# Row length of two normalised operand tiles in a float32r transformer step, 386 or 392 floats

## The reference

```python
def trunk(x, c, p):
    for li in range(DEPTH):                       # DEPTH = 2
        sh1, sc1, g1, sh2, sc2, g2 = ada_mods(c, p['w_ada'][li], p['b_ada'][li])
        h = rms_norm(x, p['norm_w'][li, 0]) * (1 + sc1) + sh1
        y = even_layer(h, ...) if li % 2 == 0 else odd_layer(h, ...)
        x = x + g1 * y
        h = rms_norm(x, p['norm_w'][li, 1]) * (1 + sc2) + sh2
        x = x + g2 * (jnp.square(jax.nn.relu(h @ p['w_mlp1'][li])) @ p['w_mlp2'][li])
```

## Time and profile before

| | |
|---|---|
| Median of 3 runs | 1049.16 us |
| Runs | 1047.77 to 1050.31 us |
| Span of the profiled execution | 1047.8 us |
| Its time outside the span | not shown by the page |
| PE busy in the span | 1020.6 us, 97% |
| DVE, ACT, POOL busy | 568.5, 486.1, 140.8 us |
| DMA | 160.44 MB, mean 153 GB/s |
| TensorE clock granted, mean | 0.994 |

### The profile page before, as it was taken

How to read it: one execution, slowest core, us unless ns; L and a number is a source line. 1 busy time by engine, 2 the same in 40 slices (tenths; PEclk the granted TensorE clock), 3 DMA queues, 4 the chain that set the end, 5 groups by cost and what they waited for, 6 DMA issues and landing times.

```text
span 1047.8 us, 17863 instructions
## 1 busy us (share of the span) xinstructions
PE 1020.6 (97%) x7330; PEld 941.7 (90%) x7330; DVE 568.5 (54%) x914; ACT 486.1 (46%) x858; POOL 140.8 (13%) x173
## 2 busy tenths in 40 slices
PE   6999999999999999999999999999999999999997
PEld 3888885778999999999997989886999999999997
DVE  5556676564744345354457576576465445345452
ACT  5544665664553342342344556667464234252342
POOL 0162200011010010110110342350001011010110
PEclk9999999999999999999999999998999999999999
DMA  9987719645435445445445532223223524333311
GB/s 330 343 283 244 237 48 322 202 162 195 152 121 167 155 161 161 161 159 162 153 129 186 176 104 68 86 87 101 80 81 121 162 92 149 120 120 120 121 41 61
DMA packets 156974, 160.44 MB, mean 153 GB/s; under 512 B 3146, under 2 KB 155108, under 8 KB 156900
## 3 DMA queue, kind: packets, MB, share of 16 engines
q1 hardware_dynamic: 154512, 156.15, 45.0%
q0 software_dynamic: 704, 1.97, 0.6%
q10 hardware_dynamic: 1684, 1.26, 0.4%
HBM read 156.09 MB, written 3.28 MB: 152 GB/s over the span
## 4 chain that ended last, share of the span: by engine, by line
PE 92%; DVE 3%; ACT 2%; issue 1%; DMA 1%; SPq 0%; DVEq 0%; ACTq 0%
PE G L585 63%; PE G L590 13%; PE OB L607 4%; PE TB L554 4%; PE SC L918 2%; PE OB L932 1%; PE SC L694 1%; DMA raw<-in_w_ada 1%; PE OB L715 1%; PE OB L785 1%; PE TB L900 1%; ACT wH L1024 1%; PE SC L670 1%; PE SC L664 1%; PE SC L626 1%
## 5 line engine op out<-in xcount | busy, mean ns | idle before, releaser
L585 PE MATMUL G<-opH,wH 128*128 128x386 f32 (+1 forms) x768 | 267.7, 349 | 1.1 <-DVE wL L1505 0.8
L1024 ACT ACTIVATE wH<-raw 128x2048 fp32r<-128x2048 f32 x94 | 179.6, 1911 | 180.9 <-PE G L585 178.1
L585 PE MATMUL G<-opH,wL 128*128 128x386 f32 (+1 forms) x768 | 260.4, 339 | 0.0
L585 PE MATMUL G<-opL,wH 128*128 128x386 f32 (+1 forms) x768 | 260.2, 339 | 0.0
L1505 DVE TENSOR_TENSOR wL<-raw,wH 128x2048 fp32r<-128x2048 f32 x94 | 215.8, 2296 | 42.9 <-ACT wH L1024 42.9
L585 PE MATMUL G<-hidH,wH 128*128 128x384 f32 x512 | 173.3, 338 | 0.0
L585 PE MATMUL G<-hidH,wL 128*128 128x384 f32 x512 | 172.1, 336 | 0.0
L585 PE MATMUL G<-hidL,wH 128*128 128x384 f32 x512 | 172.1, 336 | 0.0
L585 PEld LDWEIGHTS G<-opH,wH 128*128 128x128 f32 x768 | 144.9, 189 | 9.8 <-issue 5.4
L585 PEld LDWEIGHTS G<-opL,wH 128*128 128x128 f32 x768 | 144.8, 189 | 1.6
L585 PEld LDWEIGHTS G<-opH,wL 128*128 128x128 f32 x768 | 144.9, 189 | 0.0
(11 more groups left out here) (246 smaller groups left out, 1192.6 us busy)
## 6 DMA issues: line engine op xcount, KB each, us to landing
raw<-in_w_mlp SPq DMA_DIRECT2D x64, 1024.0 KB, 5.2
raw<-in_w_ada SPq DMA_DIRECT2D x48, 1024.0 KB, 7.0
raw<-in_w_in_even SPq DMA_DIRECT2D x13, 1024.0 KB, 7.2
raw<-in_w_in_odd SPq DMA_DIRECT2D x12, 1024.0 KB, 5.1
raw<-in_w_out_even SPq DMA_DIRECT2D x4, 1024.0 KB, 6.6
raw<-in_w_out_odd SPq DMA_DIRECT2D x4, 1024.0 KB, 5.0
xin<-in_x_sample SPq DMA_DIRECT2D x2, 512.0 KB, 5.7
out_y_sample<-yout SPq DMA_DIRECT2D x1, 768.0 KB, 4.1
```

Source lines behind the costliest of these rows:

```text
L585: mm = pe.matmul(G[:, s, 512 * m:512 * m + cols], w[:, s, k, P * m:P * m + P], a[:, k, 0:cols], start=first and q == 0, stop=last and q == 2)
L1024: act.activation(wH[:, u % 2, :, :], raw[:, pos % RAW, :, :], ACT.Copy).then_inc(w_high, 1)
```

## The change

The two tiles get rows of 392 floats, 1568 bytes, which is 49 times 32. Every row of `opH` and `opL` then begins at a multiple of 32 bytes. The last six floats of a row are never written or read. `opL` begins 192 bytes later than before, all that is declared behind it 384 bytes later. No instruction is added or removed, and no shape changes.

```diff
 NX = NTOK + 2
+ROW = 392
...
-        opH = sb("opH", [P, KT, NX], F32R)
-        opL = sb("opL", [P, KT, NX], F32R)
+        opH = sb("opH", [P, KT, ROW], F32R)
+        opL = sb("opL", [P, KT, ROW], F32R)
```

## The result

The changed kernel takes 1052.2 us, the median of 20 runs (1050.26 to 1055.1), against 1049.39 us for 20 runs of the kernel before beside it (1045.38 to 1053.25): a ratio of 1.0028, 95% interval 1.0019 to 1.0038. It is slower by 2.9 us, where 1045.0 was forecast. Its profiled execution has a span of 1048.1 us.

The account below looks back on a forecast made before the run. TensorE, busy 97% of the span, was taken as the bound through the pace between matmul starts. Gains of 1.8 + 0.8 + 1.6 = 4.2 us took 1049.2 to 1045.0 us, range 1042.7 to 1047.4.

Parts of the forecast that it names:

- pieces of 32 bytes: Matmul pace on TensorE: a streamed row costs 3.61 ns for each 32-byte piece it touches, taken from `hid` rows.
- Three paces that agree within 0.7 ns: Measured `op` paces the assumption fitted: 175.7 ns at 384 columns, 177.2 and 177.6 at 386 in layers 1 and 0.
- the sentence that was called its refutation: Irregular steps in the 384-column output projection units of the changed trace would make the prediction wrong at its root.
- Item 1: 768 matmuls of 384 columns out of `op`: from 175.7 to 173.3 ns each, a gain of 1.8 us.
- Item 3: 1224 tok matmuls, stationary tile coming into phase: half of the possible gain taken, 1.6 us.
- Item 2: 1536 matmuls of 386 columns: from 177.4 to 176.9 ns each, a gain of 0.8 us.
- Item 5: Later tiles move by 384 bytes, a multiple of 32, 64 and 128, so their phases stay: no effect.
- locked at the bad end: Rival, 386-column units: steps repeat at 180 ns instead of 177.4, costing 4.0 us less 1.8, giving 1051.4; chance 0.12.

Follow-up runs that it names:

- e3_pads: Kernel before, rows of 386 floats kept, with 192 unused bytes behind each of `opH` and `opL`; ratio 1.0001 to the kernel before.
- e12: Changed kernel with `opH`/`opL` rows 28 bytes past a multiple of 32 and `raw` 192 past a multiple of 256; ratio 0.9952 to the kernel before.
- e1: Model left out: blocks of 96 or 144 matmuls alone at various row places, a `hid` block returning between; ran once, `hid` at 173.3 or 176.7 ns.
- e2: Changed kernel with layer 1's MLP rows taken in layer 0's order, nothing else; ratio 1.0001 to the kernel before.
- e8: Model left out: matmul blocks alone, 392-float rows at eight phases, also rows of 386, 388, 390; 386 columns took 173.9 to 177.9 ns.

## Why the prediction was wrong

The bound was read rightly: TensorE's pace sets the time, and neither the other engines nor the two tiles' writers gave or took anything (`opL` 554 ns and `opH` 528 as before). The forecast failed at three steps.

**Its root: pieces of 32 bytes.** Three paces that agree within 0.7 ns were taken for a law, from one assumption and four measured numbers. The blocks alone contradict it, and the sentence that was called its refutation came true: the 384-column output units, in phase at every row, stand at 175.3 ns with uneven steps (172 to 185), not at `hid`'s 173.3. Item 1 gave 0.4 ns x 768 = 0.3 us instead of 1.8. Item 3 gave nothing: tok went from 118.2 to 118.4, a loss of 0.2 us where 1.6 were forecast. Item 2 came out as forecast by luck: from the first matmul of each group of 386-column units to the next group's, layer 0 gained 144.54 - 143.88 = 0.66 us and layer 1 138.73 - 138.64 = 0.09, 0.75 against 0.8, but for another reason, since e3_pads gains 1.6 with the old rows. The upper end of the range was off as well: its gain of 6.5 us is no sum of the items, which give 1.8 + 0.8 + 3.2 = 5.8 with all of tok's.

**Item 5, "Nothing".** The later tiles keep their phases of 32, 64 and 128, and that was where the reasoning stopped; `raw` stood on a multiple of 256 and left it. The trace of before shows `raw` filled at 386 GB/s with the DMA engines full in the prologue, the one place where TensorE's waits are put down to it, so it was a term to be bounded and not one to be struck out. It costs some 1.5 to 2 us. The Trainium skill, page "DMA: Bandwidth & Descriptors", section "How a descriptor splits into AXI transactions", says that a descriptor which does not start on a multiple of 256 bytes is split at those multiples, and that the bytes between the multiple below and its start cost as well. It speaks of what is read; here it is the place written to that moved. By its figures a 1 KB packet that starts 128 bytes past takes 36 beats instead of 32, an estimate of 343 GB/s from 386; 348 was measured, close to it. 192 bytes past it would be 38 beats and 325 GB/s, and e12 shows 348, so the trace does not agree with the figures there. By the same account both places cut a packet into one more piece than before; whether that sets the rate is not shown.

**Item 5 again: `hid` left out.** The prediction took `hid`'s 173.3 ns as what rows in phase cost, a constant. It is one of two patterns of the same instructions at the same addresses, and what runs ahead can choose between them (e1, e2). The change turned layer 1 into the other: 2.1 us, the largest term of the result beside the prologue, and no part of the sum. The rival "locked at the bad end" had the mechanism, steps that repeat at a slow value, and the right side, but put it into the 386-column units, at 180 ns; those went to 176.7. That its time, 1051.4, lies near the 1052.2 measured is luck: the loss came from other terms. The 180 ns exist (388 columns, rows of 512 floats) where no kernel here uses them.

**The sum as it came out:** a gain of 0.75 + 0.3 - 0.2 = 0.85 us in the changed units, a loss of 2.1 in `hid` and about 2 in the prologue: some 3.2 us slower, where the runs show 2.9, between 2.0 and 4.0.

**Still open.** Why a place and an entry give one pattern and not another was not found: distances between tiles, the weights' place and the rows' order all enter, and the opening blocks of e1 and e8 differ with all of these equal. Why the clock falls in some executions is open too. Of the runs with `raw` off its multiple 69 of 72 have a mean granted clock of 0.995 or less, of those with `raw` on it, the kernel before among them, 68 of 115; 0.993 or less have 51 of the 72 and 10 of the 115. So the fall comes oftener with the late transfers, but it comes without them too, and how the price of some 2 us divides between the wait and the clock was not measured.

## What to carry to other kernels

Where TensorE streams without a gap, a tile's place in SBUF is a parameter to be measured and not one to be reasoned out: run the matmuls alone at the eight phases of a row, take the fastest, and look in the model whether the streams behind it keep their pattern. Whoever changes one tile's size should list every tile declared behind it with its old and new place, up to multiples of 512 bytes, and ask of those that DMAs fill whether they left a multiple of 256. A constant read from the profile is only one where something shows that it cannot be otherwise; `hid`'s pace was the same in every undisturbed unit before, and was still one of two.

## What the runs showed of the hardware

- One stream of matmuls at the same addresses runs at 173.33 or 176.67 ns a step, depending on the block ahead of it, and once settled stays so to the end of the block, of 96 matmuls (e1: L29, L35, L37). With no block ahead it settled at either pace as well (e1 L27, e8 L34).
- Neither alignment nor fewer columns is a guide to the pace: 388 columns at 180.0 ns against 392 at 175.6 in rows of 512 floats; with 386 columns rows 28 bytes off a multiple of 32 at 173.9 to 174.5 ns, rows on it at 176.9 to 177.3. The fastest pace of a whole block at 384 columns was 173.3 ns.
- 1 KB packets into a tile that starts 128 or 192 bytes past a multiple of 256 move 348 GB/s instead of 386, 51 to 52 ns a packet where it was 46.
